# Last rows of the third and fourth down projections, and where the gate's first weights are rounded

## What is computed

```python
def swiglu(x, w1, w3, w2):
    return (jax.nn.silu(x @ w1) * (x @ w3)) @ w2

for i in range(DEPTH):                      # second block, DEPTH = 2
    mix = mixer_mla_sb(...) if i % 2 == 0 else mixer_fox(...)
    x = layer_norm_2(DEEPNORM_ALPHA * x + mix, ln1_g[i], ln1_b[i])
    x = layer_norm_2(DEEPNORM_ALPHA * x + swiglu(x, ffn_w1[i], ffn_w3[i], ffn_w2[i]), ln2_g[i], ln2_b[i])
    x = x + jax.nn.sigmoid(x @ ple_w_gate[i] + ple_b_gate[i]) * (p[i] @ ple_w_proj[i])
```

## Time and profile before

| | |
|---|---|
| median of 3 runs | 1428.86 us (1427.92 to 1429.13) |
| the profiled execution: its own time | 1428.52 us |
| its span in the profile | 1426.7 us |
| TensorE busy | 1400.3 us (98%) |
| VectorE busy | 1024.2 us (72%) |
| ScalarE busy | 933.0 us (65%) |
| GpSimd busy | 384.5 us (27%) |
| `w_lo`, line 1732, 295 times | 375.7 us, 1289 ns each on average |

### The profile page before, as it was taken

One profiled execution on the slowest core, in us unless ns is written; L12 is line 12 of the kernel. 1 busy time (PEld: TensorE's weight loads), 2 busy tenths in 40 slices (PEclk: granted clock), 3 DMA queues, 4 the chain that ended last, 5 costly groups with the idle time before them and its releaser, 6 DMA issues.

```text
span 1426.7 us, 30780 instructions
## 1 busy us (share of the span) xinstructions
PE 1400.3 (98%) x11088; PEld 1345.2 (94%) x11088; DVE 1024.2 (72%) x1653; ACT 933.0 (65%) x1569; POOL 384.5 (27%) x384
## 2 busy tenths in 40 slices
PE   9999999999999999999999999999999999999998
PEld 7899889999999999999998789999999969999998
DVE  6867766888749978887588857665478775766557
ACT  5633437655976476558867757557778787655866
POOL 4343002332306313333052124212034301421203
PEclk9999999999999999999999999999999999999999
DMA  6533214555664554556645135555645614655662
GB/s 216 176 104 96 68 37 159 171 171 178 194 192 146 167 186 158 178 170 187 206 151 189 60 104 182 185 178 172 201 158 163 215 52 134 192 183 185 187 195 91
DMA packets 62728, 226.04 MB, mean 158 GB/s; under 512 B 6960, under 2 KB 8240, under 8 KB 62640
## 3 DMA queue, kind: packets, MB, share of 16 engines
q1 hardware_dynamic: 61776, 221.87, 49.4%
q10 hardware_dynamic: 864, 3.01, 0.6%
HBM read 223.80 MB, written 1.05 MB: 158 GB/s over the span
## 4 chain that ended last, share of the span: by engine, by line
PE 67%; DVE 19%; issue 6%; ACT 5%; DMA 1%; POOL 1%; DVEq 1%; SPq 0%; ACTq 0%
PE bank L414 17%; PE bank L415 17%; PE bank L416 17%; DVE w_lo L1732 8%; DVE cv L2127 2%; PE bank L459 1%; DVE tu L1783 1%; DVE x_lo L1760 1%; ACT w_hi L1114 1%; PE bank L448 1%; DVE tg L1783 1%; PE bank L452 1%; PE bank L869 1%; PE bank L871 1%; PE bank L870 1%
## 5 line engine op out<-in xcount | busy, mean ns | idle before, releaser
L414 PE MATMUL bank<-x_hi,w_hi 128*128 128x258 f32 (+5 forms) x2096 | 602.2, 287 | 6.7 <-DVE w_lo L1732 3.8
L416 PE MATMUL bank<-x_hi,w_lo 128*128 128x258 f32 (+5 forms) x2096 | 594.0, 283 | 0.0
L415 PE MATMUL bank<-x_lo,w_hi 128*128 128x258 f32 (+5 forms) x2096 | 593.4, 283 | 0.0
L414 PEld LDWEIGHTS bank<-x_hi,w_hi 128*128 128x128 f32 x2096 | 395.5, 189 | 16.6 <-issue 13.1
L1732 DVE TENSOR_TENSOR w_lo<-raw,w_hi 128x1024 fp32r<-128x1024 f32 x295 | 375.7, 1289 | 48.5 <-ACT w_hi L1114 33.6
L1114 ACT ACTIVATE w_hi<-raw 128x1024 fp32r<-128x1024 f32 x299 | 313.0, 1052 | 127.9 <-PE bank L416 104.9
L415 PEld LDWEIGHTS bank<-x_lo,w_hi 128*128 128x128 f32 x2096 | 396.1, 189 | 0.4
L416 PEld LDWEIGHTS bank<-x_hi,w_lo 128*128 128x128 f32 x2096 | 395.9, 189 | 0.0
L1730 DVE SCALAR_TENSOR_TENSOR w_lo<-raw,negmean,w_hi 128x1024 fp32r<-128x1024 f32 x120 | 157.0, 1311 | 145.1 <-ACT w_hi L1112 143.8
L416 PE MATMUL bank<-a_hi,w_lo 128*128 (+2 forms) x704 | 198.1, 281 | 0.0
L415 PE MATMUL bank<-a_lo,w_hi 128*128 (+2 forms) x704 | 197.9, 281 | 0.0
(11 more groups left out here) (453 smaller groups left out, 2222.6 us busy)
## 6 DMA issues: line engine op xcount, KB each, us to landing
raw<-w SPq DMA_DIRECT2D x419, 512.0 KB, 3.7
h<-h SPq DMA_DIRECT2D x2, 544.0 KB, 6.0
out<-h SPq DMA_DIRECT2D x8, 128.0 KB, 1.9
T<-cs ACTq DMA_DIRECT2D x1, 960.0 KB, 6.2
con_b<-cb ACTq DMA_DIRECT2D x1, 712.0 KB, 3.9
smx<-pin ACTq DMA_DIRECT2D x1, 512.0 KB, 4.8
con_g<-ca ACTq DMA_DIRECT2D x1, 421.5 KB, 6.8
prm<-par ACTq DMA_DIRECT2D x1, 202.0 KB, 4.8
```

The costliest lines, as they stand in the source:

```text
L414: pe.matmul(o, wh, xh, start=first, stop=False)
L415: pe.matmul(o, wh, xl, start=False, stop=False)
L416: return pe.matmul(o, wl, xh, start=False, stop=last)
```

## The change

It holds for n = 5 and n = 7 alone. On TensorE the row before the last is done as the rows ahead of it are, all eight banks in `DOWN_ORDER`, with its `unit_done` at its end; only the last row is done in `LAST_ORDER` with three matmuls to a bank. On ScalarE the high part of unit gate is made ahead of the norm's first `x_hi` instead of behind its last `sq`. On VectorE the low part of unit gate is made inside the norm, behind r(3) and low(2), and no longer behind low(7).

```diff
@@ TensorE, row_stage
-                for k in range(3 + RING * full, nk - 2):
+                rows = 1 if n in (5, 7) else 2
+                for k in range(3 + RING * full, nk - rows):
                     one(u0 + k, u0 + k, k)
-                ready(u0 + nk - 2, nk - 2)
+                if rows == 2:
+                    ready(u0 + nk - 2, nk - 2)
                 ready(u0 + nk - 1, nk - 1)
                 for j, m in enumerate(LAST_ORDER[n]):
-                    mm = three(*parts(u0 + nk - 2, u0 + nk - 2, nk - 2, m), False, False)
-                    if j == KT - 1:
-                        mm.then_inc(S("unit_done"), 1)
+                    if rows == 2:
+                        mm = three(*parts(u0 + nk - 2, u0 + nk - 2, nk - 2, m), False, False)
+                        if j == KT - 1:
+                            mm.then_inc(S("unit_done"), 1)
                     three(*parts(u0 + nk - 1, u0 + nk - 1, nk - 1, m), False, True).then_inc(S("bank_done"), 1)
@@ ScalarE, layer_norm
-                for j in range(2 + RING * full, nk - 2):
+                early = nk - 1 if n in (5, 7) else nk - 2
+                for j in range(2 + RING * full, early):
                     act.wait_ge(S("unit_done"), u0 + j + 1)
                     ahead(u0 + j, u0 + j)
...
-                for j in range(nk - 2, nk):
+                for j in range(early, nk):
                     act.wait_ge(S("unit_done"), u0 + j + 1)
                     ahead(u0 + j, u0 + j)
@@ VectorE, layer_norm
                     if j >= 1:
                         low(j - 1)
+                    if j == 3 and n in (5, 7):
+                        ahead(u0 + nk - 1, u0 + nk - 1)
                 low(KT - 1)
                 x_hi_n[0] += KT
-                ahead(u0 + nk - 1, u0 + nk - 1)
+                if n not in (5, 7):
+                    ahead(u0 + nk - 1, u0 + nk - 1)
                 if n not in (5, 7):
                     ahead(u0 + nk, u0 + nk)
```

## The result

The changed kernel takes 1433.37 us (median of 7 runs, 1432.24 to 1434.88), the kernel before 1427.92 us (7 runs, 1427.65 to 1429.13): +5.45 us, ratio 1.0037 with the 95% interval 1.0027 to 1.0047. It is slower by more than the 0.2% that can be told. The forecast was 1431.7, or +2.8 against the median then known (1428.86): the direction came, and nearly twice the size; the forecast had given slower by over 0.2% the chance 0.42, less than no change, 0.56. The measured median lies 0.07 above the upper end of the range, and since the kernel before came out 0.94 quicker beside it than the median that the forecast started from, the change itself, +5.45, lies further out, by 1.0: the range reached to +4.4.

The account below looks back on a forecast made before the run. TensorE was taken to bound the kernel, so the change could act only through its gaps; gate + 1 starting 1.49 us later at two places made +3.0, from which 1431.7 us was forecast, range 1429.2 to 1433.3.

Parts of the forecast that it names:

- What bounds the kernel: TensorE, busy 98% of the span; gaps ahead of gate + 1 behind `down2` and `down3` hold about 1.4 us each.
- The banks come 0.89 later: Last row of the down projection: its first bank is final later, so VectorE begins r(0) of the norm 0.89 later.
- The first `x_hi` behind the early `w_hi`: ScalarE, start of the norm: `x_hi` waits for gate's `w_hi`, costing 0.11 more, so low(0) to low(2) come 1.00 later.
- The moved `w_lo` and GpSimd's hold: VectorE, inside the norm: `w_lo` takes 1.17 and GpSimd's addition holds it out 0.49, so r(4) is 2.66 later.
- The pace behind it: VectorE, r(4) to r(7) behind the moved `w_lo`: stays at 0.88 a bank.
- rival (a): In the norm, `w_lo` beats GpSimd's addition (0.49 a stage back) or last banks go faster (up to 0.6); chance 0.25.
- The term of the gap: TensorE at the gate: starts on gate + 1 1.49 later at each of the two places.
- The sum "2 stages x 1.49, and nothing else": Whole kernel: the later starts on gate + 1 add +3.0 us, and nothing else adds to the time.
- rival (b): In the norm, GpSimd keeps VectorE out twice, holding low(3) and low(4): +1.1 a stage at most, 1433.9; chance 0.15.
- The ceiling on a gain, 2.8 us: The two gaps ahead of gate + 1: no mechanism inside the change can give back more than 2.8 us.
- Rivals (b) to (d): (b) has its line; (c) norm without waits or hold, 1426.5, chance 0.02; (d) finish not moved, at least 1429.3, chance 0.10.

Follow-up runs that it names:

- filled run: Changed kernel with 11 matmuls, whose results nothing reads, put into TensorE's idle stretch ahead of gate + 1 at both places: 1430.83 us.
- reordered kernel: Kernel before, with gate's 16 matmuls by the high parts of x and the sum of squares ahead of gate + 1's: 1426.84 us; same edit on changed kernel 1427.88.
- the fourth place alone: The change made only at the fourth down projection (n = 7), the third as in the kernel before: 1430.94 us, +3.16.
- the first four experiments: The four follow-up experiments measured first; beside them the kernel before took 1427.78 us (31 runs).
- the third place alone: The change made only at the third down projection (n = 5), the fourth as in the kernel before: 1430.65 us, +2.87.

## Why the prediction was right or wrong

**What bounds the kernel: right in the place, wrong in one step.** The loss arose at the two places named, and the start of gate + 1 is what counted: letting TensorE do other work there took the gap away. But "a change that neither adds nor removes matmuls can act only through the gaps" did not hold. The same 11088 matmuls kept TensorE busy 1.5 us longer in the profiled execution, and about half of the loss is matmuls made longer by the low clock.

**The banks come 0.89 later: right**, 0.81 net of proj in the run with TensorE's part alone. That proj itself would be 0.20 shorter was in no row.

**The first `x_hi` behind the early `w_hi`: right**, to 0.02.

**The moved `w_lo` and GpSimd's hold: right**, 1.68 from its start to that of r(4), 1.66 forecast (1.17 + 0.49), and shown by the run with `w_lo` ahead of the additions. The rule of the Trainium skill ("SBUF — State Buffer", section "SBUF: two separate sides") that the prediction laid beside it, that the hold lasts for the whole instruction, here 0.75 less the 0.07, would have made the `w_lo` some 0.15 longer than it is; that the one which starts first keeps the other out is as it says.

**The pace behind it: nearly.** One of the three steps from r(4) to r(7) was 0.72 and not 0.88, part of rival (a), worth 0.13 a place.

**The term of the gap: right in size.** 1.49 a place was forecast; from proj to gate + 1 it is 1.59, net of the quicker proj 1.39, 2.8 us for both, as the filled run measured (+2.80).

**The sum "2 stages x 1.49, and nothing else": wrong.** "Nothing else" is the step that failed. I read the granted clock in the earlier trace rows, nines in every slice, and took it for a given, though my own forecast put an idle stretch of nearly 3 us where the trace of before had none longer than 1.4. A row of before could not price that; it ought to have been a rival that adds to the forecast. It cost 2.65 us in the median: the changed kernel less the filled one. With it the forecast of 3.0 becomes 5.65, against 5.45 measured. That the measured time lies so near the upper end of the range is luck: rival (b), which did not come, had set that end, and no term for the clock.

**The ceiling on a gain, 2.8 us: not tested by the change**, since it lost. The reordered kernel suggests that the ceiling was too high even so: at the first place part of a gain comes back as a wait in the next layer. Of rival (a) only the quicker step came, 0.13 of its 0.6 a place. Rivals (b) to (d) didn't come.

## What to carry to other kernels

Moving a wait from in front of a chain into it pays only if what it holds up inside is not on the path: here every part of the change put the norm later by more than it took away behind it. Where a forecast makes an idle stretch on TensorE longer than any that the trace shows, the clock belongs in the sum as a term of its own, and a full clock in the profile of before says nothing on it. And when TensorE waits for one of two weight units, it can do first all that the other allows: here that took 1.19 us off the kernel before (interval up to no change) and 5.6 off the changed one.

## What the runs showed of the hardware that I had not expected

- The clock falls within a kernel whose TensorE is 98% busy. Behind an idle stretch of 2.8 us the clock was at 0.50 from 1052 to about 1057.6 in one place of the changed kernel and stayed at 1.00 behind an equal stretch in the other, and that other place had the low clock in the kernel with the fourth place alone. With two waits of 1.36 and 0.63, and two matmuls between them, it fell too. It cost 2.69 and 2.70 us in two of the profiled executions and 1.53 to 1.56 in three. In the kernel before, 25 of the 31 runs beside the first four experiments have a mean clock of 0.999 or more (1426.95 to 1428.20 us), the six others 0.998 (1428.25 to 1428.94); the stretch at 36 us, low in three of the profiled executions (the filled kernel, TensorE's part alone and the third place alone) and full in that of the kernel before, may be the place, but none of the six was profiled.
- The same 48 matmuls of proj take 5.33 us when the row before the last is done by itself and 5.53 when the last two rows are done bank by bank, each time, at both places (5.34 and 5.53 in the kernel with the third place alone), with the granted clock at 1.00. I have no cause for it.
